# Loading and splitting the first two weight groups of seven projections one block earlier

## The reference

```
q, k, v = split(h @ wqkv, 3)          # h: 768 tokens (512 + 256 context)
y = attend(q, k, v) @ wo              # layer 0: differential attention, layer 1: neighbourhood attention
x = x + gate1 * y
x = x + gate2 * conv_ffn(norm(x))
```

```
proj = concat(hc, hx) @ w_in
y = (sigmoid(g1) * (dn @ w_dn) + sigmoid(g2) * (hg @ w_hg)) @ w_out
x = x + gate1 * y
x = x + gate2 * hier_moe(norm(x))
```

## Time and profile before

| | |
|---|---|
| median of 3 runs | 4015.16 us (4011.31 to 4016.72) |
| profiled execution | 3999.07 us, span 3997.3 us |
| TensorE busy | 3411.1 us, 85% of the span |
| VectorE busy | 2249.4 us, 56% |
| ScalarE busy | 1489.2 us, 37% |
| GpSimd busy | 317.9 us, 8% |
| mean granted TensorE clock | 0.935 of full speed |
| DMA | 525.71 MB, mean 132 GB/s |

### The profile page before, as it was taken

The page is one execution under the profiler, slowest core; times in us unless marked ns, Lnnn a source line. Parts: engine busy times, 40 slices in busy tenths (PEclk is TensorE's granted clock), DMA queues, the critical chain, the costliest instruction groups (busy, mean ns, idle before and its releaser), DMA issues. The chain is left out here.

```text
span 3997.3 us, 48930 instructions
## 1 busy us (share of the span) xinstructions
PE 3411.1 (85%) x18626; PEld 2720.9 (68%) x18626; DVE 2249.4 (56%) x2870; ACT 1489.2 (37%) x1934; POOL 317.9 (8%) x203
## 2 busy tenths in 40 slices
PE   5988988999997898799997778879876876999994
PEld 3885666888885887577875567758654664666662
DVE  4538735656554147377754245455642226888884
ACT  4014713212122046342324333323322225777772
POOL 0000010000000000200001125201103310000000
PEclk8999989999998999999998888989987987999997
DMA  4640013443431211256631160011012236999993
GB/s 156 220 153 1 1 42 105 136 151 128 150 108 53 63 48 38 64 183 197 191 111 42 30 205 0 10 43 43 1 42 63 74 133 234 379 391 385 387 384 114
DMA packets 362840, 525.71 MB, mean 132 GB/s; under 512 B 14944, under 2 KB 300256, under 8 KB 338144
## 3 DMA queue, kind: packets, MB, share of 16 engines
q1 hardware_dynamic: 355360, 498.99, 36.6%
q10 hardware_dynamic: 5056, 16.80, 1.1%
q0 software_dynamic: 2304, 8.39, 0.6%
HBM read 484.81 MB, written 39.32 MB: 131 GB/s over the span
## 5 line engine op out<-in xcount | busy, mean ns | idle before, releaser
L252 DVE TENSOR_TENSOR lo<-exp_raw,exp_hi 128x2048 fp32r<-128x2048 f32 x192 | 436.2, 2286 | 100.0 <-ACT exp_hi L2897 99.2
L2897 ACT CAST exp_hi<-exp_raw 128x2048 fp32r<-128x2048 f32 x192 | 366.5, 1912 | 155.7 <-DMA exp_raw<-in_w_experts 87.0
L245 PE MATMUL ffn_acc<-normed_hi,up_w_hi 128*128 128x512 f32 (+1 forms) x1056 | 378.7, 359 | 26.4 <-DVE lo L252 25.9
L247 PE MATMUL ffn_acc<-normed_hi,lo 128*128 128x512 f32 (+1 forms) x1056 | 377.3, 357 | 0.0
L246 PE MATMUL ffn_acc<-lo,up_w_hi 128*128 128x512 f32 (+1 forms) x1056 | 377.0, 357 | 0.0
L245 PE MATMUL feat_acc<-normed_hi,feat_w_hi 128*128 128x512 f32 (+1 forms) x544 | 204.4, 376 | 65.9 <-DVE lo L252 65.6
L245 PEld LDWEIGHTS ffn_acc<-normed_hi,up_w_hi 128*128 128x128 f32 x1056 | 199.1, 188 | 65.0 <-issue 20.4
L425 DVE SCALAR_TENSOR_TENSOR aside_w<-aside_w,aside_c 128x1024 f32<-128x1024 f32 x192 | 229.0, 1220 | 20.9 <-DMA aside_w<-in_ada_t 19.3
L246 PEld LDWEIGHTS ffn_acc<-lo,up_w_hi 128*128 128x128 f32 x1056 | 199.9, 189 | 31.6
L247 PEld LDWEIGHTS ffn_acc<-normed_hi,lo 128*128 128x128 f32 x1056 | 199.0, 188 | 29.9
L245 PE MATMUL ffn_acc<-gated_hi,down_w_hi 128*128 128x512 f32 (+1 forms) x528 | 191.5, 363 | 13.1 <-DVE lo L252 12.8
(11 more groups left out here) (504 smaller groups left out, 8552.4 us busy)
## 6 DMA issues: line engine op xcount, KB each, us to landing
exp_raw<-in_w_experts SPq DMA_DIRECT2D x192, 1024.0 KB, 10.6
aside_w<-in_ada_t SPq DMA_DIRECT2D x192, 512.0 KB, 6.2
up_w<-in_ffn_up SPq DMA_DIRECT2D x88, 512.0 KB, 5.1
x_rows<-dn_zero SPq DMA_DIRECT2D x42, 384.0 KB, 5.2
exp_x<-x_rows SPq DMA_DIRECT2D x32, 384.0 KB, 6.7
y_rows<-exp_y ACTq DMA_DIRECT2D x32, 384.0 KB, 7.9
ada_w<-in_ada_first SPq DMA_DIRECT2D x8, 1024.0 KB, 9.9
feat_w<-in_a_wqkv SPq DMA_DIRECT2D x16, 512.0 KB, 4.3
```

The costliest lines, as they stand in the source:

```text
L245: nc.tensor.matmul(out, left[0], right[0], start=start, stop=False)
L247: return nc.tensor.matmul(out, left[1], right[0], start=False, stop=stop)
L252: return engine.tensor_tensor(lo, value, hi.bitcast(F32), ALU.subtract)
L2897: nc.scalar.copy(hi[r][:], raw[u * TILES + j][:]).then_inc(tile_hi[j], 1)
```

## The change

A new class `Ahead` holds two weight tiles with their `hi` and `lo` and can load them (on SP) and split them, either on VectorE (`split`) or with the cast on ACT (`high`) and the subtraction on GpSimd (`low`). For seven projections the object is made before the block that precedes, this block loads and splits the first two groups, and the projection starts with them:

- `token_rows` of both layers, `gated_rows`, and the k `features` of layer 1: the `features` block ahead issues the two loads after its own last one and VectorE splits them after its own last split. In layer 0 they stand behind the `Aside` loads, which have all been issued by then, and ahead of VectorE's `biases`.
- the three `residual` blocks: `differential`, `neighbourhood` and `merge` issue the loads as SP's first instructions. ACT casts them after step 6 of `differential`, after step 4 of `neighbourhood`, and before the last pair of `merge`; GpSimd subtracts them, in `merge` after its own work.

In those projections the wait for the first two groups is gone (`w_split` is raised once per tile at the block's start, or the wait is left out), and the loads and splits run from the third group on. In `token_rows` of layer 0 the `Aside` loads and takes now start at once.

Memory for it: the weight tiles of `features` in layer 0, of the k `features` in layer 1 and of the HGRN2 `features`, and two of the four `Aside` tiles in layer 0, are laid into `v` or `fi` (`room`). The products and their order are unchanged.

```diff
-    def __init__(self, K, ctx, ring, weights, *segments):
+    def __init__(self, K, ctx, ring, weights, *segments, room=None):
...
-        self.tile = [K.sb(ctx, f"aside_w{u}", [P, D]) for u in range(ring)]
+        spare = [room[:, n, :] for n in range(4, NT)] if room is not None else []
+        self.tile = [K.sb(ctx, f"aside_w{u}", [P, D]) for u in range(ring - len(spare))] + spare
...
+class Ahead:
+    def __init__(self, K, ctx, name, shape, *sources, room=None):
+        self.K, self.sources = K, sources
+        if room is None:
+            self.raw = [K.sb(ctx, f"{name}_w{u}", shape) for u in range(2)]
+            self.hi = [K.sb(ctx, f"{name}_w_hi{u}", shape, FR) for u in range(2)]
+            self.lo = [K.lo(t) for t in self.raw]
+        else:
+            rounded = K.lo(room)
+            tile = lambda t, n: t[:, n, 0:KD * P].rearrange("p (c n) -> p c n", c=KD)
+            self.raw, self.lo, self.hi = ([tile(t, n + u) for u in range(2)] for t, n in ((room, 0), (rounded, 0), (rounded, 2)))
+        self.full = [K.sem(f"{name}_ahead_full") for _ in range(2)]
+        self.hi_done = [K.sem(f"{name}_ahead_hi") for _ in range(2)]
+    def load(self, sp):
+        for u in range(2):
+            sp.dma_start(self.raw[u][:], self.sources[u]).then_inc(self.full[u], 16)
+    def split(self, dve):
+        for u in range(2):
+            dve.wait_ge(self.full[u], 16)
+            self.K.nc.vector.tensor_copy(self.hi[u][:], self.raw[u][:]).then_inc(self.hi_done[u], 1)
+            dve.wait_ge(self.hi_done[u], 1)
+            lo_of(self.K.nc.vector, self.lo[u][:], self.raw[u][:], self.hi[u][:])
+    def high(self, act):
+        for u in range(2):
+            act.wait_ge(self.full[u], 16)
+            self.K.nc.scalar.copy(self.hi[u][:], self.raw[u][:]).then_inc(self.hi_done[u], 1)
+    def low(self, pool):
+        for u in range(2):
+            pool.wait_ge(self.hi_done[u], 1)
+            lo_of(self.K.nc.gpsimd, self.lo[u][:], self.raw[u][:], self.hi[u][:])
...
-def features(K, h, w, segments, tok, evac, first=None, aside=None):
+def features(K, h, w, segments, tok, evac, first=None, aside=None, early=None, following=None, room=None):
...
-        wt = [K.sb(ctx, f"feat_w{u}", [P, KD, P]) for u in range(2)]
-        wh = [K.sb(ctx, f"feat_w_hi{u}", [P, KD, P], FR) for u in range(2)]
-        wl = [K.lo(t) for t in wt]
+        own = early or Ahead(K, ctx, "feat", [P, KD, P], room=room)
+        wt, wh, wl = own.raw, own.hi, own.lo
...
+                if following:
+                    following.load(sp)
                 side.load(sp, side.count)
...
-            split(0)
+            if early:
+                for u in range(2):
+                    dve.sem_inc(w_split[u], 1)
+            else:
+                split(0)
...
+                if following:
+                    following.split(dve)
                 side.take(dve, side.count)
                 side.biases(dve)
                 return
             with dve.Fori(0, n_chunks // 2 - 1) as it:
-                split(it + 1)
+                split(it if early else it + 1)
+            if following:
+                following.split(dve)
...
-def residual(K, src, w, gate_at, tok):
+def residual(K, src, w, gate_at, tok, early):
...
         def _(act):
-            for n in range(KD):
-                act.wait_ge(w_full[n % 2], n // 2 * 16 + 16)
+            for n in range(2, KD):
+                act.wait_ge(w_full[n % 2], (n // 2 - 1) * 16 + 16)
                 nc.scalar.copy(wh[n % 2][:], wt[n % 2][:]).then_inc(w_hi[n % 2], 1)
...
-            with pool.Fori(0, KD // 2) as it:
+            for u in range(2):
+                pool.sem_inc(w_split[u], 1)
+            with pool.Fori(0, KD // 2 - 1) as it:
...
+        @block.sync
+        def _(sp):
+            following.load(sp)
+
+        @block.gpsimd
+        def _(pool):
+            following.low(pool)
...
                 take(g)
                 if g >= 1:
                     outputs(g - 1)
+                if g == NT:
+                    following.high(act)
...
-def merge(K, h, w_in, dn, w_dn, hg, w_hg, m):
+def merge(K, h, w_in, dn, w_dn, hg, w_hg, m, following):
...
         @block.sync
         def _(sp):
+            following.load(sp)
             with sp.Fori(0, KD // 2) as it:
...
+            following.low(pool)
...
+            following.high(act)
             pair(KD // 2 - 1, False)
```

More of the change, by code:

```diff
@@ L3118, in second_block @@
                 h = normed(proj, True, True)
+                ahead = Ahead(K, proj, "gr", [P, KD, 256], *columns_of(w_in, C_HF, 256))
                 features(K, h.parts, w_in, ((C_HQ, HEADS),), TX,
-                         lambda n, sums: nc.scalar.activation(q[:, at(n), :], sums, ACT.Silu), first=h)
-                gated_rows(K, h.parts, w_in, fi, kk)
+                         lambda n, sums: nc.scalar.activation(q[:, at(n), :], sums, ACT.Silu), first=h, following=ahead, room=fi)
+                gated_rows(K, h.parts, w_in, fi, kk, ahead)
             hgrn(K, q, fi, kk, ohg, io["spans"])
@@ L3132, in second_block @@
         m = K.sb(ctx, "merged", [P, KD, TX])
-        merge(K, h.parts, w_in, dn, io["w_br_dn_2"][0], hg, io["w_br_hg_2"][0], m)
-        residual(K, m, io["w_out_2"][0], 16, TX)
+        ahead = Ahead(K, ctx, "res", [P, KD, P], *columns_of(io["w_out_2"][0], 0, P))
+        merge(K, h.parts, w_in, dn, io["w_br_dn_2"][0], hg, io["w_br_hg_2"][0], m, ahead)
+        residual(K, m, io["w_out_2"][0], 16, TX, ahead)
     with ExitStack() as ctx:
```

115 lines of the change are left out of this document (67 added, 48 removed).

## The result

The changed kernel took 3969.32 us (median of 4 runs, 3967.35 to 3974.84), the kernel before beside it 4013.23 us (4010.71 to 4016.72). The ratio is 0.9892, with a 95% interval from 0.9875 to 0.9909: 43.9 us faster. Forecast were 3971.4 us and 43.8 us.

A forecast was written before the change was run, and what follows sets the result against it. TensorE's waits at seven starts on a serial load, split and product chain were the bound: 54.85 us less slips of 0.2 and 1.7, less costs of 9.2, leaves 43.8, so 3971.4 us; range 3955 to 3991.

The forecast's parts named there:

- the 0.66 taken from the earlier trace: Time from the last evacuation's end to TensorE's first product where no source has to be split: 0.66 us.
- A: Start of token_rows in layer 0: TensorE restarts at 220.1 instead of 229.15, gaining 9.05 us.
- C: Start of the second (k) features of layer 1: restart at 1290.83 instead of 1296.77, gaining 5.95 us.
- B: Start of token_rows in layer 1, with the same chain as in layer 0: gaining 8.95 us.
- the clock's part: Products after the restarts of token_rows, k features and gated_rows keep the higher clock: 1.6 us each, 6.4 us in all.
- the slip of 0.2: Layer 0's features block ends later because token_rows' preloads and splits finish late: 0.2 us lost (0 to 2).
- G: Start of gated_rows: restart at 2654.1 instead of 2662.83, gaining 8.7 us before its slip.
- G's slip: The features block ahead of gated_rows ends later, waiting for the second preloaded group's split: 1.7 us lost (0 to 4).
- D: residual of layer 0 (768 tokens): second group starts at 541.8 instead of 545.12, gaining 3.3 us.
- E: residual after neighbourhood in layer 1 (512 tokens): first group ends at 1639.3 against 1644.85, gaining 5.5 us.
- F: residual after merge: first group ends at 3197.0 against 3204.04, gaining 7.0 us.
- attention absorbs everything: Rival: differential and neighbourhood take up the added work without loss, gain 49.4 us, 3965.8 us; chance 0.10.

The follow-up runs named there:

- the three residuals alone: Kernel before with only the three residual blocks starting on preloaded groups, the four projections left as before: 3994.92 us, ratio 0.9960.
- the four projections alone: Kernel before with preloaded groups only at both token_rows, the k features and gated_rows; residual, attention and merge blocks as before: 3973.53 us, ratio 0.9907.
- the two partial runs: Two kernels each with one part of the change against the kernel before: only the four projections (3973.53 us), only the three residual blocks (3994.92 us).
- the second measurement: The changed kernel, unaltered, measured and profiled once more beside the kernel before: 3961.53 us, ratio 0.9882, 45.8 us faster.

## Why the prediction was right, point by point

**The bound.** The serial chain of load, split and product was the whole of the idle time at the seven places; taking it away gave what its length said. The restart came a little later than the 0.66 taken from the earlier trace rows: 223.44 - 222.65 = 0.79 at A, 0.93 at C. That is 0.1 to 0.3 each. Counted from the copy's end the start at A, C and B gained 8.92, 5.67 and 8.85 us, where 9.05, 5.95 and 8.95 were forecast.

**A stage that took longer.** A falls 1.0 short. The restart is 0.1 of it and the clock's part 0.3; the slip of 0.2 that was taken off didn't come. 0.75 is `features` itself, 142.5 us to its last product against 141.7 before. Here is a pair of its copies before, then a pair after:

```profile
201.94 0.80 ACT L1511 COPY qk<-feat_acc 128x768 f32 x1 [7.54 <-PE feat_acc L247]
210.29 0.80 ACT L1511 COPY qk<-feat_acc 128x768 f32 x1 [7.55 <-PE feat_acc L247]
```

```profile
205.06 0.80 ACT L1591 COPY qk<-feat_acc 128x768 f32 x1 [7.60 <-PE feat_acc L247]
213.46 0.80 ACT L1591 COPY qk<-feat_acc 128x768 f32 x1 [7.60 <-PE feat_acc L247]
```

A chunk takes 213.46 - 205.06 = 8.40 us instead of 210.29 - 201.94 = 8.35, and so do all from the second to the last, 15 of them: 0.75. It is 8.40 in all twelve profiles with the changed stage, and 8.35 in the two without it (before, and the three residuals alone). The k `features` of layer 1 have the same two paces, which makes 0.4 us in C. The clock isn't the cause: how much of the lower clock falls into the first chunk moves the stage by another 0.7 us, from 141.0 to 141.7 without the change and from 141.8 to 142.5 with it. Nor is it VectorE's added splits, since the kernel with only the loads ahead has 8.40 as well, or these loads, since the pace is there from the second chunk on, long before them. What is left is the new place of the tiles, in `v`, or the changed program around them. The prediction put this term at nothing ("have the same shapes and cost nothing"), and that step failed, by 0.75 + 0.4 us. Which of the two it is wasn't tried.

**The clock.** The gain came at A, B and C, with 1.28 and 1.29 us (`token_rows` at A and B) and 1.28 (k `features` at C, 1.7 without its slower pace), where 1.6 each were forecast, and didn't come at G (-0.2). Against the run of the three residuals alone, where these starts are as before, it is 2.6, 1.9 and 2.4 us and 1.1 at G: a trace of before has more or fewer products at the lower clock (12 at A in one, 25 in the other), and 1.6 lies between. The prediction said that the gaps are near the limit at G, and the step that failed is to have counted it all the same: 1.6 of the 6.4. What it rested on was the clock read while TensorE stood idle. That can't tell what comes behind, as the idle time at G shows:

```profile
2627.70:2630.20 2.50, 0.00 (x0) 0.01 (x1) 2.21 (x1) 0.62 (x2) 0.00 (x0) 1.00 0.00 0
```

The clock still reads 1.00 there, and 0.51 in the 3 us from the restart on.

**G's slip.** Forecast 1.7, measured 1.5 (2629.91 against 2628.40). The run with both splits earlier gives it back in full, and the clock's part with it.

**D.** Forecast 3.3, measured 538.67 against 546.27 before, less the 3.40 us by which the stage's first cast moved: 4.2. Here the term was mis-sized by a misread row. The second group before did not start at 545.12. That row, is the first product of the eighth chunk. The second group's first product is this row of before:

```profile
546.27 0.40 PE L245 MATMUL res_acc<-res_hi,res_w_hi 128*128 128x512 f32 x1
```

With it the same working gives 546.27 - 541.8 = 4.5. The pitch of 1.46 us and the end of the contention were as said.

**E and F.** Forecast 5.5, measured (1644.85 - 1630.02) - (1617.04 - 1607.59) = 5.4. Forecast 7.0, measured 6.9 in the same way, of which 0.4 is lost again before it: VectorE's idle time ahead of its first cast is 0.88 us instead of 0.50. At E the clock was at 0.58, and as said TensorE caught up with VectorE.

**The attention stages.** Forecast 3.5 in `differential`; the stage grew by 3.8, which looks like a hit. But 1.8 of it arose before the first cast, in a stretch that also differs where nothing was changed, and what the added work cost is 2.0. For `neighbourhood` 2.1 was forecast and 0.6 measured in the same way (1.2 with the start). The stalls were partly taken up, as the rival "attention absorbs everything" has it: 2.6 of 5.6 us cost. The rule of the Trainium skill named in the prediction gave about 3.4 for both blocks and was nearer than my sum.

**`merge`.** Forecast 3.6 for the first product, measured 3.58. But the stage was forecast to be as long as before from then on. In the first profile its first group took 19.6 us instead of 18.35, at the lower clock; in the second it took 18.35 again. In both TensorE stands 0.2 to 0.4 us longer ahead of the third, fifth and seventh group than before, 0.8 and 1.0 us together. But that isn't the change in `merge`: in the run of the four projections alone, whose `merge` is as before, it is 0.9. It is once more the one trace of before that is short.

**The other rivals.** None of the landings came late: at B and C TensorE waits for no weights. The barrier cost the 1.7 us that the earlier trace rows had let expect. The sum of the stages is 39.5 to 41.8 against 43.8. The short fall is the clock's part (1.8 at G, 0.6 at A, B and C), the slower `features` (1.15), the restarts (about 0.5) and F (0.9 to 2.9), against gains at D (1.0) and E (0.7) and about 1 us in smaller pieces. Against the untouched stages of the two partial runs the sum is 44.7 to 47.0, so how far the stages stand from the medians, 43.9 and 45.8, lies within what one trace of before leaves open. That the forecast met the first median within 0.1 us is luck: its terms are off by up to 2.9 us each, both ways, and the second measurement is 2.0 us away.

## What to carry to other kernels

Where blocks are parted by barriers, the first weights of the next block belong into the one ahead, behind its own last load; load and split should both end before that block's last evacuation, and if VectorE has gaps earlier in the block, the split goes into them. A residue of one or two microseconds at such a place can cost more than its length: the clock fell behind it at G, and the pace of the whole following stage went with it. Where such an edit's parts are to be judged, compare stage by stage, since within 0.2% the medians of differently laid out programs don't tell. But take more than one trace of the kernel before, and look at the stages that you didn't touch: here they moved by 2.5 to 2.7 us together between two traces, which is as much as some of the parts were worth.

## What was not expected of the hardware

- The same products at the same granted clock of 1.00 run at 117.8 or at 113.3 ns, for the whole of a stage of some 100 us. It went with how the stage began (after 2.55 us of idleness or more in ten profiles, after 1.04 in four), but each kernel had one pace only. That is 5.4 us of `gated_rows`. The reason is open.
- In the same way a chunk of `features` in layer 0 takes 8.35 us in two profiles and 8.40 in the twelve other profiles, at a granted clock of 1.00 and with the same products.
- At A and B the clock held over an idle time of TensorE of 1.71 to 1.74 us each time and over 1.75 in two kernels. It fell behind 1.75 in a third, behind 1.79 and 1.90 (all at A), and behind 2.55 to 2.60 each time (G). At A that alone moved `token_rows` by 1.5 us from one kernel to another.
- GpSimd's subtraction held up a VectorE instruction on one value per partition until its own end: 0.22 became 2.01 us, and about 2.01 in each of the nine profiles with these subtractions in `differential`.
- One execution's profile lay 14 us below its kernel's median, with a stage that nobody touched (the normalisation ahead of layer 1's `features`) at 21.8 us against 24.7 in twelve of the thirteen others.
